# First attention layer of a diffusion trunk: the query's quarter swap goes from VectorE to small SBUF transfers, and the chunk products are spread anew

## The chip, the core and the metric

One NeuronCore of one Trainium2 chip runs the whole program. The metric is the device time of one execution in microseconds. Three runs of the kernel before took 2476.61 to 2477.92 us, median 2477.8. The engines are named as in the profile: PE (TensorE matmul), PEld (its weight load), DVE (VectorE), ACT (ScalarE), POOL (GpSimd), SP (SyncE). SPq and ACTq are the DMA issues of SP and ACT.

## The reference, cut to what matters

The trunk has four layers over 256 latent and 256 context tokens with 1024 features, in f32. Layer 0 and layer 3 are differential attention, layer 1 retention, layer 2 neighbourhood attention, and each is followed by a SwiGLU feed-forward. The change touches the mixer of layer 0:

```python
def axial_rope(x, rows, cols):
    ...
    x1, x2 = x32[..., : d // 2], x32[..., d // 2:]
    return jnp.concatenate([x1 * cos - x2 * sin, x1 * sin + x2 * cos], axis=-1).astype(x.dtype)

def diff_attention(hx, hz, w_qkv, w_o, lam_p, subln_g, lam_init, rows, cols, need_ctx):
    ...
    qx = axial_rope(qx, rows, cols)
    kx = axial_rope(kx, rows, cols)
    ...

def _diff_core(q, k, v, lam, scale):
    s = jnp.einsum('bqnd,bknd->bnqk', q, k).astype(F32) * scale
    p = jax.nn.softmax(s, axis=-1)
    b, n, tq, tk = p.shape
    p = p.reshape(b, n // 2, 2, tq, tk)
    a = p[:, :, 0] - lam * p[:, :, 1]
    return jnp.einsum('bhqk,bkhe->bqhe', a.astype(v.dtype), v)
```

Each head has 64 features, so the rotation pairs feature p with feature p +- 32. Beside it the modulation `silu(cond) @ w_ada + b_ada` is needed (`ada_mod`): 48 chunks of 128 outputs for each layer, each for the latent and for the context condition.

## The kernel before, in words

Features lie on the 128 partitions, tokens on the free axis (columns 0 to 255 latent, 256 to 511 context). Every weight matrix comes as "units" of 128x1024 values (512 KB) through a ring of four slots: SP loads `w_raw` (L420), ACT rounds it to `w_hi` (L1198), POOL subtracts to `w_lo` (L589), PE multiplies three times (hi*hi, hi*lo, lo*hi) per 128x128 block, so one unit at 512 columns is 24 matmuls.

Attention of layer 0 runs in eight tiles t of 128 features (two heads and their differential partner). For each tile PE computes the query unit into bank 6 and the key unit into bank 7, turns the weights of tile t-1 (`turn`), multiplies them with the values (`weighted`, copies by ACT L1389), and then scores tile t (`score`, six banks in the order 0, 1, 2, 4, 5, 3). Between them stands `mean_square` of tile t-1, and the last score needs a bank that DVE frees with `subnorm` of tile t-1 (L2044, semaphore `y_ready`).

DVE's order in a tile is written out by hand (`tile_da`): weights of t-1 (`weights_`, L2022 to L2037), rotation of q, rotation of k, row maxima of the scores (L2009, L2012), `subnorm` and `low` of t-1. A rotation (`rotate`, L1983) is four multiplies of 32 partitions each (L1987), which take the query from PSUM at the swapped partitions and write `rot`, one multiply of 128 partitions in PSUM (L1990) and one add into `qT` or `kT` (L1991). ACT's order is: exponentials of t-1, `value_rows`, the copy of the query's context half into `qT` (L1439), the same for the key (L1442, when PE has done the key unit), the copies of the turned weights, two weight units (`ahead`), and `high` of t-1.

In the gaps of this order DVE also works off the modulation products of layer 0 (`rest_products`, L1733): chunks 16 to 39, two products each, 48 in all, each over 128x1024 values, followed at group ends by a small sum (`ada_sums`, L1668). `ADA_VALUES`, `ADA_TILE`, `ADA_TAIL` and `ADA_PROJECT` say how many stand where; `ADA_GROUPS` says which chunk is loaded into which slot and together with which others. SP issues these loads between the weight loads (L434, `ada_rest_load`).

ACT issues two more transfers in this layer: after tile 0 the small table `rpb_rows` (L1465), and after tile 1 `rpb_skew` (L1470), which writes the table 64 times over into DRAM for the bias of layer 2, in rows of 508 bytes.

After the tiles comes the output projection (`project`): five units at 512 columns, then three units on the latent half alone, and then the same three on the context half, each of which waits until DVE has added the residual of its latent half (`x_new`, L1763).

Of the kernel before, what the change touches and what calls it, by code (L numbers as in the profile page):

```python
# [20 lines left out]
ALU = mybir.AluOpType  # L21
# [32 lines left out]
ADA_GROUPS = ((16, 0, (16, 17, 0, 4, 1, 5)), (22, 1, (2, 6, 3, 7)), (26, 0, (3,)), (27, 1, (7, 20, 21)),  # L54
              (30, 0, (3, 7)), (32, 1, (20, 21, 22)), (35, 0, (20, 23)), (37, 1, (12, 13, 14)))
ADA_MIXER = 40
ADA_VALUES = 4
ADA_TILE = ((0, 1, 2), (1, 1, 1), (1, 1, 2), (1, 1, 2), (1, 1, 2), (1, 1, 2), (1, 1, 2), (1, 1, 2))
ADA_TAIL = 8
ADA_PROJECT = (1, 1, 1, 1, 1, 1)  # L60
LOOPED = 4
# [80 lines left out]
class Layer:  # L142


    def __init__(self, sem, li, first_unit):
# [10 lines left out]
        self.first = (5 if self.kind != 1 else 6) if self.zq else KT  # L156
        self.half_done = sem(f"half_done_{li}")
        self.v_done = sem(f"v_done_{li}")
        self.v_act = sem(f"v_act_{li}")
        self.v_dve = sem(f"v_dve_{li}")  # L160
        self.s_done = sem(f"s_done_{li}")
        self.osq_ready = sem(f"osq_ready_{li}")
        self.oms_done = sem(f"oms_done_{li}")
        self.ors_ready = sem(f"ors_ready_{li}")
        self.y_ready = sem(f"y_ready_{li}")
# [12 lines left out]
        else:  # L178
# [5 lines left out]
            self.a_ready = sem(f"a_ready_{li}")  # L184
            self.t_done = sem(f"t_done_{li}")
            self.aT_ready = sem(f"aT_ready_{li}")
            self.vst_ready = sem(f"vst_ready_{li}")
# [44 lines left out]
def trunk(nc, xT_in, cond_in, weights, ada_w, ada_b, gains, final_g, lam_in, subln_in, decay_in,  # L232
          rpb_in, da_rope_in, ret_rope_in, ret_exp_in, na_mask_in, ident_in, out, layers=DEPTH):
    with ExitStack() as ctx:
# [173 lines left out]
        def _(sp):  # L408
# [99 lines left out]

            sp.wait_ge(plan[0].pv_done, KT)
            ada_rest_load(7)  # L510

            def bias_load(L, t, slot, reused):
# [667 lines left out]
        def _(act):  # L1180
# [162 lines left out]
            def attention(L):  # L1343
# [86 lines left out]
                def tile_da(t, c, i, place):  # L1430
# [6 lines left out]
                    if L.zq:  # L1437
                        act.wait_ge(unit_used, t * 2 + (n + 1))
                        nc.scalar.activation(qT[:, SEQ:TOK], bank[6][:, SEQ:TOK], ACT.Copy, scale=DA_DIM ** -0.5)\  # L1439
                            .then_inc(L.qk_act, 1)  # L1440
                    act.wait_ge(unit_used, t * 2 + (n + 2))
# [201 lines left out]
        def _(dve):  # L1643
# [339 lines left out]
            def rotate(src, dst, table):  # L1983
# [7 lines left out]
                return V.tensor_tensor(out=dst, in0=src, in1=rot[:, :], op=ALU.add)  # L1991

            def attention(L, e0):
                n = L.n + KT
# [81 lines left out]

                def tile_da(t, place, extra=(0, 0, 0)):
                    if place:
                        rest_products(extra[0])
                        weights_(t - 1)  # L2080

                    dve.wait_ge(unit_used, t * 2 + (n + 1))
                    if L.zq:
                        dve.wait_ge(L.qk_act, t * 2 + 1)
                    rotate(bank[6][:, 0:SEQ], qT[:, 0:SEQ], 0).then_inc(L.qk_dve, 1)
                    rest_products(extra[1])
                    dve.wait_ge(L.qk_act, t * (1 + L.zq) + (1 + L.zq))

                    dve.wait_ge(L.qk_dve, t * 2 + 1)
                    rotate(bank[7][:, 0:SEQ], kT[:, 0:SEQ], 2).then_inc(L.qk_dve, 1)  # L2090
                    rest_products(extra[2])
                    maxima(t, 0, range(2))
                    if place:
                        subnorm(t - 1, da_banks(L)[0])
                    maxima(t, 0, range(2, L.banks))
                    if place:
                        low(t - 1, da_banks(L)[0])
# [14 lines left out]
                else:  # L2112
                    tile_da(0, 0)
                    tile_da(1, 1)
                    with own.loop((KT - 2) // 2, 2 * (1 + 4)) as i:
                        for s in range(2):
                            tile_da(i * 2 + (2 + s), 1)
                weights_(KT - 1)
                if L.li == 0:
                    rest_products(ADA_TAIL)  # L2120
                subnorm(KT - 1, LAST_O)
# [305 lines left out]
```

## Time and profile before

| | us |
|---|---|
| median of 3 runs | 2477.8 |
| the profiled execution | 2478.16 |
| its span, first to last instruction | 2476.4 |
| PE busy in the span | 2417.1 (98%) |
| DVE busy | 1276.4 (52%) |
| ACT busy | 999.6 (40%) |
| POOL busy | 1111.5 (45%) |
| mean granted clock | 0.995 |
| tiles 0 to 7 of layer 0's attention | about 84 to 254 |
| its projection, up to the feed-forward | about 254 to 309 |

PE is busy nearly everywhere, but the shares are a mean over stages. In layer 0's attention DVE is nearly as full as PE. The slices of the page show DVE at 0.8 to 0.9 for the first 300 us and at 0.1 to 0.7 later. The granted clock is given as a share of full speed: 1.00 is 2.4 GHz and 0.50 is 1.2 GHz.

### The profile page before, as it was taken

How to read it: one execution, taken by the hardware profiler on the slowest of the kernel's cores; microseconds unless marked ns; L12 is line 12 of the kernel's file. 1: busy time of each engine (PE TensorE's matmuls, PEld its weight loads, DVE VectorE, ACT ScalarE, POOL GpSimd, SP SyncE). 2: the span in 40 equal slices, each digit the busy share in tenths (PEclk: the TensorE clock that was granted, in tenths of full speed). 3: DMA queues.
4: the chain of work that ended last, by engine and by line, in shares of the span. 5: the costliest groups of instructions: out<-in, count | busy, mean ns of one | idle time of the engine just before them, and what ended most of it. 6: DMA issues, size and time to landing. Idle time of an engine off the chain costs nothing.

```text
span 2476.4 us, 37125 instructions
## 1 busy us (share of the span) xinstructions
PE 2417.1 (98%) x12236; PEld 1976.8 (80%) x12236; DVE 1276.4 (52%) x2243; ACT 999.6 (40%) x2004; POOL 1111.5 (45%) x839
## 2 busy tenths in 40 slices
PE   8999999999999999999999999999999999998998
PEld 3566788888887777788888887778888888777998
DVE  8988876647233322247664243665666424465211
ACT  3466442332333332333323244664323324465553
POOL 0432444445443334334445434223544544435996
PEclk9999999999999999999999999999999999999999
DMA  8363345546322222235555324222555532322654
GB/s 338 111 102 110 126 163 203 199 166 222 104 87 77 74 70 86 84 103 204 189 187 192 115 73 111 78 84 94 203 203 197 184 104 92 96 75 89 192 186 128
DMA packets 119715, 340.61 MB, mean 138 GB/s; under 512 B 35537, under 2 KB 40401, under 8 KB 118993
## 3 DMA queue, kind: packets, MB, share of 16 engines
q1 hardware_dynamic: 111602, 333.97, 41.1%
q10 hardware_dynamic: 8032, 5.52, 1.5%
q8 instruction: 55, 0.90, 0.2%
q14 instruction: 26, 0.21, 0.0%
HBM read 334.76 MB, written 4.69 MB: 137 GB/s over the span
## 4 chain that ended last, share of the span: by engine, by line
issue 45%; PE 32%; POOL 18%; DVE 2%; DMA 1%; ACT 1%; SPq 1%; POOLq 1%; DVEq 0%; ACTq 0%
PE low_banks L596 28%; POOL w_lo L589 18%; PE high_banks L596 4%; DVE tmp L1804 1%; DVE h_lo L1812 0%; DMA ada_first<-in_ada_w 0%; DMA w_raw<-in_weights 0%; ACT w_hi L1198 0%; POOLq L588 0%; DVE ssum_rstd L1660 0%; POOLq L583 0%; SPq L466 0%; SPq L420 0%; DVE dump L1680 0%; SPq L434 0%
## 5 line engine op out<-in xcount | busy, mean ns | idle before, releaser
L589 POOL TENSOR_TENSOR w_lo<-w_raw,w_hi 128x512 fp32r<-128x512 f32 x832 | 1111.1, 1362 | 1345.8 <-ACT w_hi L1198 1345.2
L596 PE MATMUL low_banks<-h_hi,w_hi 128*128 128x512 f32 (+1 forms) x1792 | 644.1, 359 | 12.2 <-DVE h_lo L1812 8.4
L1198 ACT ACTIVATE w_hi<-w_raw 128x512 fp32r<-128x512 f32 x832 | 474.1, 624 | 418.3 <-PE low_banks L596 209.7
L596 PE MATMUL low_banks<-h_lo,w_hi 128*128 128x512 f32 (+1 forms) x1792 | 634.5, 354 | 0.0
L596 PE MATMUL low_banks<-h_hi,w_lo 128*128 128x512 f32 (+1 forms) x1792 | 634.4, 354 | 0.0
L596 PEld LDWEIGHTS low_banks<-h_hi,w_hi 128*128 128x128 f32 x1792 | 339.8, 190 | 68.7 <-issue 13.3
L1660 DVE SCALAR_TENSOR_TENSOR ssum_rstd<-ada_raw,high_banks 128x1024 f32<-128x1024 f32 x304 | 370.7, 1219 | 41.8 <-DMA ada_raw<-in_ada_w 32.9
L596 PEld LDWEIGHTS low_banks<-h_lo,w_hi 128*128 128x128 f32 x1792 | 340.0, 190 | 47.6 <-issue 1.9
L596 PEld LDWEIGHTS low_banks<-h_hi,w_lo 128*128 128x128 f32 x1792 | 339.9, 190 | 46.2
L1572 ACT ACTIVATE lnm<-low_banks 128x512 f32<-128x512 f32 (+1 forms) x88 | 47.8, 543 | 429.6 <-PE low_banks L596 429.5
L2250 DVE TENSOR_TENSOR tmp<-low_banks,lnm 128x512 f32<-128x512 f32 (+1 forms) x88 | 55.0, 625 | 290.0 <-ACT lnm L1572 286.3
L596 PE MATMUL high_banks<-h_hi,w_hi 128*128 128x512 f32 (+1 forms) x384 | 147.9, 385 | 1.1 <-DVE qT L1991 1.1
L596 PE MATMUL high_banks<-h_lo,w_hi 128*128 128x512 f32 (+1 forms) x384 | 144.0, 375 | 0.0
L596 PE MATMUL high_banks<-h_hi,w_lo 128*128 128x512 f32 (+1 forms) x384 | 143.6, 374 | 0.0
L596 PE MATMUL high_banks<-u_hi,w_hi 128*128 128x256 f32 (+1 forms) x424 | 141.2, 333 | 0.5 <-POOL w_lo L589 0.5
L596 PE MATMUL high_banks<-u_hi,w_lo 128*128 128x256 f32 (+1 forms) x424 | 140.6, 332 | 0.0
L596 PE MATMUL high_banks<-u_lo,w_hi 128*128 128x256 f32 (+1 forms) x424 | 140.5, 331 | 0.0
L596 PE MATMUL low_banks<-u_hi,w_lo 128*128 (+2 forms) x352 | 127.8, 363 | 0.0
L596 PE MATMUL low_banks<-u_lo,w_hi 128*128 (+2 forms) x352 | 127.8, 363 | 0.0
L596 PE MATMUL low_banks<-u_hi,w_hi 128*128 (+2 forms) x352 | 127.8, 363 | 0.0
L1763 DVE SCALAR_TENSOR_TENSOR xT<-high_banks,mod,xT 128x256 f32<-128x256 f32 x52 | 24.6, 479 | 174.2 <-PE high_banks L596 174.0
L2255 DVE TENSOR_TENSOR u_lo<-tmp,u_hi 128x512 f32 (+2 forms) x88 | 65.9, 749 | 60.8 <-ACT u_hi L1577 56.0
(246 smaller groups left out, 3691.9 us busy)
## 6 DMA issues: line engine op xcount, KB each, us to landing
w_raw<-in_weights SPq DMA_DIRECT2D x424, 512.0 KB, 3.7
ada_raw<-in_ada_w SPq DMA_DIRECT2D x152, 512.0 KB, 3.9
ada_first<-in_ada_w SPq DMA_DIRECT2D x24, 512.0 KB, 9.6
ada_rest<-in_ada_w SPq DMA_DIRECT2D x9, 512.0 KB, 7.6
bias<-rpb_skew SPq DMA_DIRECT2D x64, 64.0 KB, 2.4
v_all<-in_ada_w SPq DMA_DIRECT2D x7, 512.0 KB, 6.1
rpb_skew<-rpb_rows ACTq DMA_DIRECT2D x1, 3556.0 KB, 31.7
cond_l<-in_cond SPq DMA_DIRECT2D x3, 1024.0 KB
```

The source lines that it names most:

```text
L589: nc.gpsimd.tensor_tensor(out=w_lo[:, r, part], in0=w_raw[:, r, part], in1=w_hi[:, r, part], op=ALU.subtract).then_inc(lo_ready, 1)
L596: return nc.tensor.matmul(dst, lhsT, rhs, start=start, stop=stop, **kw)
L1198: nc.scalar.activation(w_hi[:, r, part], w_raw[:, r, part], ACT.Copy).then_inc(hi_ready, 1)
L1572: nc.scalar.activation(lnm[:, 0:L.W], bank[2 * s][:, 0:L.W], ACT.Silu)\
L1660: last = V.scalar_tensor_tensor(out=dump, in0=w, scalar=1.0, in1=cond[:, c, :], op0=ALU.mult, op1=ALU.mult, accum_out=ada_sum[:, r, c:c + 1])
L1763: return V.scalar_tensor_tensor(out=x, in0=src[:, COLS[c]], scalar=gate_of(L, which, m, c), in1=x, op0=ALU.mult, op1=ALU.add)
L1804: V.scalar_tensor_tensor(out=tmp[:, m % 2, COLS[c]], in0=xT[:, m, COLS[c]], scalar=amp[:, L.par, q % 2, m, c:c + 1], in1=rstd[:, COLS[c]], ...
L2250: V.tensor_tensor(out=tmp[:, s, 0:L.W], in0=bank[2 * s + 1][:, 0:L.W], in1=lnm[:, 0:L.W], op=ALU.mult).then_inc(L.u_free, 1)
L2255: V.tensor_tensor(out=row(u_lo, j, L.W), in0=tmp[:, s, 0:L.W], in1=row(u_hi, j, L.W), op=ALU.subtract).then_inc(L.u_lo_ready, 1)
```

## The change

In layer 0, and there only, ACT now copies all 512 columns of the query out of PSUM, scaled, into `qT`, waits for its own copy, and issues four transfers within SBUF, of 32 partitions x 256 f32 (32 KB) each, that write the swapped latent half into `rot`. DVE waits for all four (`swapped_in`) and then rotates with three operations on SBUF operands in place of six. The key's rotation stays. The 48 chunk products are spread differently, chunks 37 to 39 go to other slots, and their loads are tied to other events. A few semaphores that nobody used are dropped.

```diff
-              (30, 0, (3, 7)), (32, 1, (20, 21, 22)), (35, 0, (20, 23)), (37, 1, (12, 13, 14)))
+              (30, 0, (3, 7)), (32, 1, (20, 21, 22)), (35, 0, (20, 23)), (37, 1, (21, 22)), (39, 0, (20,)))
-ADA_VALUES = 4
-ADA_TILE = ((0, 1, 2), (1, 1, 1), (1, 1, 2), (1, 1, 2), (1, 1, 2), (1, 1, 2), (1, 1, 2), (1, 1, 2))
-ADA_TAIL = 8
-ADA_PROJECT = (1, 1, 1, 1, 1, 1)
+ADA_VALUES = 3
+ADA_TILE = ((0, 0, 1, 1), (1, 1, 1, 0), (1, 1, 1, 1), (1, 1, 1, 1), (1, 1, 1, 1), (1, 1, 1, 1), (1, 1, 1, 2),
+            (1, 1, 1, 2))
+ADA_TAIL = (1, 9)
+ADA_PROJECT = (1, 1, 1, 1, 0, 0)
...
-            sp.wait_ge(plan[0].pv_done, KT)
+            sp.wait_ge(ada_done, 35)
             ada_rest_load(7)
+
+            sp.wait_ge(ada_done, 36)
+            ada_rest_load(8)
...
                     if L.zq:
                         act.wait_ge(unit_used, t * 2 + (n + 1))
-                        nc.scalar.activation(qT[:, SEQ:TOK], bank[6][:, SEQ:TOK], ACT.Copy, scale=DA_DIM ** -0.5)\
-                            .then_inc(L.qk_act, 1)
+                        nc.scalar.activation(qT[:, :], bank[6][:, :], ACT.Copy, scale=DA_DIM ** -0.5).then_inc(L.qk_act, 1)
+
+                        act.wait_ge(L.qk_act, t * 2 + 1)
+                        for quarter in range(4):
+                            a, b = 32 * quarter, 32 * (quarter ^ 1)
+                            act.dma_start(rot[a:a + 32, :], qT[b:b + 32, 0:SEQ]).then_inc(L.swapped_in, 16)
...
+            def rotate_swapped(x):
+
+                V.tensor_tensor(out=rot[:, :], in0=rot[:, :], in1=da_rope[:, 3, :], op=ALU.mult)
+                own(V.tensor_tensor(out=x, in0=x, in1=da_rope[:, 2, :], op=ALU.mult))
+                return V.tensor_tensor(out=x, in0=x, in1=rot[:, :], op=ALU.subtract)
...
-                def tile_da(t, place, extra=(0, 0, 0)):
+                def tile_da(t, place, extra=(0, 0, 0, 0)):
                     if place:
                         rest_products(extra[0])
                         weights_(t - 1)
-
-                    dve.wait_ge(unit_used, t * 2 + (n + 1))
+                    rest_products(extra[1])
                     if L.zq:
-                        dve.wait_ge(L.qk_act, t * 2 + 1)
-                    rotate(bank[6][:, 0:SEQ], qT[:, 0:SEQ], 0).then_inc(L.qk_dve, 1)
-                    rest_products(extra[1])
+                        dve.wait_ge(L.swapped_in, t * 64 + 64)
+                        rotate_swapped(qT[:, 0:SEQ]).then_inc(L.qk_dve, 1)
+                    else:
+                        dve.wait_ge(unit_used, t * 2 + (n + 1))
+                        rotate(bank[6][:, 0:SEQ], qT[:, 0:SEQ], 0).then_inc(L.qk_dve, 1)
+                    rest_products(extra[2])
                     dve.wait_ge(L.qk_act, t * (1 + L.zq) + (1 + L.zq))
                     ...
-                    rest_products(extra[2])
+                    rest_products(extra[3])
                     maxima(t, 0, range(2))
...
+                if L.li == 0:
+                    rest_products(ADA_TAIL[0])
                 weights_(KT - 1)
                 if L.li == 0:
-                    rest_products(ADA_TAIL)
+                    rest_products(ADA_TAIL[1])
```

## Rows read from the trace of the kernel before

**Rows 1.** Busy time of each engine in one stretch: PE, PEld, DVE, ACT, POOL, clock, DMA.

```profile
150.00:172.00 22.00, 20.87 (x90) 14.27 (x89) 19.46 (x36) 14.00 (x34) 6.91 (x4) 1.00 0.26 83
```

**Rows 2.** DVE's timeline, tile 3 and the start of tile 5: start, duration, [idle before].

```profile
149.55 1.72 DVE L1987 TENSOR_TENSOR rot<-high_banks,da_rope 32x256 f32<-32x256 f32 x4
151.30 0.43 DVE L1990 TENSOR_TENSOR high_banks<-high_banks,da_rope 128x256 f32<-128x256 f32 x1
151.77 0.42 DVE L1991 TENSOR_TENSOR qT<-high_banks,rot 128x256 f32<-128x256 f32 x1
152.11 1.22 DVE L1733 SCALAR_TENSOR_TENSOR dump<-ada_first,cond 128x1024 f32<-128x1024 f32 x1
...
154.16 1.72 DVE L1987 TENSOR_TENSOR rot<-high_banks,da_rope 32x256 f32<-32x256 f32 x4 [0.82 <-DVE dump L1733]
...
158.68 2.16 DVE L1733 SCALAR_TENSOR_TENSOR dump<-ada_first,cond 128x1024 f32<-128x1024 f32 x1
...
162.09 0.74 DVE L2044 SCALAR_TENSOR_TENSOR tmp<-low_banks,subln,ssum_rstd 128x512 f32<-128x512 f32 x1
...
193.16 1.22 DVE L1733 SCALAR_TENSOR_TENSOR dump<-ada_first,cond 128x1024 f32<-128x1024 f32 x1 [4.22 <-DMA v_all<-in_ada_w]
```

**Rows 3.** ACT's timeline in tile 3: the query's and the key's copy.

```profile
148.59 0.36 ACT L1439 ACTIVATE qT<-high_banks 128x256 f32<-128x256 f32 x1
153.69 0.39 ACT L1442 ACTIVATE kT<-high_banks 128x256 f32<-128x256 f32 x1 [4.74 <-PE high_banks L596]
```

**Rows 4.** Timelines of PE and PEld: scores, query units, the projection's stop.

```profile
113.89 2.08 PE L596 MATMUL low_banks<-kT,qT 64*128 64x512 f32 x4 [2.25 <-DVE kT L1991]
...
136.08 1.13 PE L596 MATMUL low_banks<-kT,qT 64*128 64x512 f32 x4
...
142.47 0.19 PEld L596 LDWEIGHTS high_banks<-h_hi,w_hi 128*128 128x128 f32 x1 [0.76 <-POOL w_lo L589]
...
162.89 1.12 PE L596 MATMUL low_banks<-kT,qT 64*128 64x512 f32 x2 [1.13 <-DVE tmp L2044]
...
185.55 2.07 PE L596 MATMUL low_banks<-kT,qT 64*128 64x512 f32 x2 [2.27 <-DVE tmp L2044]
...
187.54 0.29 PEld L596 LDWEIGHTS high_banks<-h_hi,w_hi 128*128 128x128 f32 x1 [1.50 <-issue]
...
254.28 0.19 PEld L596 LDWEIGHTS high_banks<-y_hi,w_hi 128*128 128x128 f32 x1 [0.76 <-issue]
...
298.71 0.58 PE L596 MATMUL low_banks<-y_hi,w_hi 128*128 128x256 f32 x1 [3.46 <-DVE xT L1763]
```

**Rows 5.** ACT's own transfers in this layer: start and issue; KB, us to landing.

```profile
119.92 0.71 ACTq L1470 DMA_DIRECT2D rpb_skew<-rpb_rows  x1
...
rpb_skew<-rpb_rows ACTq DMA_DIRECT2D x1, 3556.0 KB, 31.7
...
rpb_rows<-in_rpb ACTq DMA_DIRECT2D x1, 13.6 KB, 1.8
```

**Rows 6.** DMA issues of the first 20 us, with KB and us to landing.

```profile
da_rope<-in_da_rope ACTq DMA_DIRECT2D x1, 512.0 KB, 7.1
...
logit<-in_decay SPq DMA_DIRECT2D x1, 4.0 KB, 14.1
```

**Rows 7.** DMA queue of ACT, 148 to 150 us: packets, MB, share.

```profile
q10 hardware_dynamic: 31, 0.01, 3.9%
```

**Rows 8.** Busy time and clock in a stretch after PE's stop at 183 to 185 us.

```profile
189.00:192.00 3.00, 3.00 (x9) 2.33 (x8) 0.00 (x0) 1.59 (x5) 0.00 (x0) 0.50 0.99 339
```

**Rows 9.** DVE adds of 128x256 on SBUF, POOL idle, then POOL at work.

```profile
299.13 0.43 DVE L1792 TENSOR_TENSOR ssum_rstd<-ssum_rstd,tmp 128x256 f32<-128x256 f32 x1
...
307.70 1.51 DVE L1792 TENSOR_TENSOR ssum_rstd<-ssum_rstd,tmp 128x256 f32<-128x256 f32 x1
```

**Rows 10.** DVE in the projection: one of the last products, and the sum.

```profile
289.80 2.31 DVE L1733 SCALAR_TENSOR_TENSOR dump<-ada_rest,cond 128x1024 f32<-128x1024 f32 x1
...
296.10 1.10 DVE L1668 TENSOR_TENSOR mod<-ada_sum,bias_ada 128x6 f32<-128x6 f32 x1
```

More of the change, by code:

```diff
@@ L156, in __init__ @@
         self.first = (5 if self.kind != 1 else 6) if self.zq else KT
-        self.half_done = sem(f"half_done_{li}")
+        if self.zq:
+            self.half_done = sem(f"half_done_{li}")
         self.v_done = sem(f"v_done_{li}")
@@ L161, in __init__ @@
         self.s_done = sem(f"s_done_{li}")
-        self.osq_ready = sem(f"osq_ready_{li}")
-        self.oms_done = sem(f"oms_done_{li}")
-        self.ors_ready = sem(f"ors_ready_{li}")
+        if self.kind != 2:
+            self.osq_ready = sem(f"osq_ready_{li}")
+            self.oms_done = sem(f"oms_done_{li}")
+            self.ors_ready = sem(f"ors_ready_{li}")
         self.y_ready = sem(f"y_ready_{li}")
@@ L185, in __init__ @@
             self.t_done = sem(f"t_done_{li}")
+            if self.kind == 0 and self.zq:
+                self.swapped_in = sem(f"swapped_in_{li}")
             self.aT_ready = sem(f"aT_ready_{li}")
```

## The prediction, made before the change was run

> **What bounds the kernel now.** I read the page first: PE is busy 98% of the span, so a change to DVE's work pays only where PE waits for DVE. The busy times by stretch show where that can be: in the middle of layer 0's attention DVE is busy 19.46 of 22 us beside PE's 20.87 [rows 1]. Then I read the timelines of that stage engine by engine, with S for the start of a tile's query unit on PE. Tile 3 has S = 142.47, and the tile's last score runs at 162.89 after a stop of 1.13 us for DVE's `subnorm`; it takes 1.05 us, so the next S is 163.94 and a tile lasts 21.47 us. From 187.54 to the projection's first unit at 254.28 there are three tiles in 66.74 us where 3 x 21.47 = 64.4 would do, and from 142.47 to 187.54 two tiles in 45.07 us where 42.9 would do [rows 4]. The excess of 2.3 and 2.1 us belongs to two events. In tile 4 a stop of 2.27 us was followed by half the granted clock [rows 4, 8]. In tile 5 a product of chunk 27 waited 4.22 us for its load [rows 2]. The stop of 1.13 us had no such sequel. Last, the projection has one stop of 3.46 us, for the residual that DVE adds late [rows 4].
>
> **The quarter swap on DVE.** It removes four multiplies of 32 partitions (1.72 us), keeps one multiply (0.43) and one add (0.42), and adds one multiply of 128x256 [rows 2]. All three operands are now in SBUF. Such an add took 0.43 us with POOL idle and 1.51 with POOL at work [rows 9]. POOL is idle when tiles 1 to 7 rotate the query, so I take three times 0.43 = 1.3 us in place of 2.6, and up to 3.3 us in tile 0.
>
> **The swap as a path.** In tile 3 ACT starts the query's copy at S + 6.1 [rows 3]. At 512 columns I take 0.6 us for it (twice the columns of the 0.36 row, less its fixed part). Then four issues; the large transfer on this queue took 0.71 us to issue [rows 5], and I take 0.4 for a small one, an estimate. From issue to landing the small table took 1.8 us [rows 5]. So the last swap lands at about S + 6.7 + 1.2 + 1.8 = S + 9.7. No transfer of this shape, SBUF to SBUF, is in the trace: below 1.8 us is open, above it I go to 4 us. DVE has meanwhile done the product that used to follow, waits 1.4 us, rotates until S + 11.0, does one product (1.22) and is at the key at S + 12.3, where it used to start at 154.16 = S + 11.7 because the key unit ends there [rows 2, 3]. The key's rotation ends at about S + 14.9, and PE's scores begin at S + 15.1. That fits just. One product less then stands before the maxima, `subnorm` comes 0.9 us earlier, and the next S is at 20.5 rather than 21.47. What was moved beside it is only ACT's wait for its own copy, behind which the key's copy is queued; ACT sat idle 4.74 us before that one [rows 3], so it costs nothing in tiles 2 to 7.
>
> **Tile 2, the term that decides.** After tile 1 ACT issues `rpb_skew` at 119.92. It lands 31.7 us later, at 151.6 [rows 5], and 31 packets of it were still served between 148 and 150 us [rows 7]. Tile 2's four swaps are issued at about 128 on the same queue, q10. The first 20 us show what a queue does to a small transfer behind large ones: 4 KB on SP's queue took 14.1 us to land, while 512 KB issued after it on ACT's queue took 7.1 [rows 6]. So a queue serves in order, and the other queue goes past it. The Trainium skill says so too (page "DMA: Bandwidth & Descriptors", section "Queues, rings and completion order"): each engine takes a ring's descriptors in order, and ACT has one row of rings.
>
> By this the swaps land at about 151.8, not at 130. DVE then needs 1.35 + 1.25 + 2.65 us for the query, a product and the key: 157.1. PE's scores start there, where they started at 136.08 [rows 4]: 21.1 us late. DVE has nothing else to do, since the wait stands ahead of everything in its order; PE goes through turn and weighted sums until 136 and then stands still. Where the clock fell after a stop it was 0.50, that is 1.2 GHz [rows 8]. In tile 1, after 2.25 us, four scores' row lasts 2.08 us where tile 2's lasts 1.13, and in tile 4 the scores' row 2.07 [rows 4], with the unit behind it still at 0.50 [rows 8]: one to some three us each. I take 1.2, since much of what follows waits on ACT and DVE in any case: +22.3, between +19 and +26.
>
> **Tiles 0 and 1.** One product fewer ahead of tile 0 pays for the swap's latency; tile 1's swap lands after DVE is free, and the key is ready at the same time as before. -0.3, between -1.5 and +2.
>
> **Tiles 3 to 5.** The product of chunk 27 moves from ahead of the weights to behind the query's rotation, later than its landing, so the 4.22 us go; with one product less before the maxima the stop of tile 4 falls below the 2.27 that halved the clock. From 142.47 to the start of tile 6, 68.8 us in all, become three times 20.5 and 0.6 for a sum: -6.7, between -7.3 and -2.
>
> **Tiles 6 and 7.** Here two products remain before the maxima while the key is ready 0.6 us later, and in tile 6 a sum falls between them, which beside POOL took 1.10 us in place of 0.17 [rows 10]. The stop grows from 1.13 to about 2, or 2.8 with the sum, where the clock may fall. +2, between +1.2 and +4.9.
>
> **Tail and loads.** Nine products in place of eight, and the last two of them wait for a group of loads that can only start when chunk 34 is done (about 6 us to land, 5 us of products in between). PE has 0.7 us to spare. +0.4, between 0 and +1.5. SP's queue gets one wait more, with nothing due behind it until the projection.
>
> **Projection.** Two products of 2.31 us and the late sum of 1.10 no longer stand before the last residuals [rows 10]. That is 4.6 us and more against a stop of 3.46 us with 2.3 us of half clock behind it [rows 4]; what is late next is PE's own third half unit. -4.3, between -5 and -2.
>
> **Sum.** 22.3 - 0.3 - 6.7 + 2.0 + 0.4 - 4.3 = +13.4 us. The profiled execution took 2478.16 us, 0.4 above the median of the runs, so 2491.6 for it and 2491.2 for the median. I say 2491. The other layers are unchanged: layer 3 has no context queries and takes the old rotation.
>
> **Rivals.**
> *The transfers pass each other.* If the swap of tile 2 didn't wait for `rpb_skew`, tile 2 would gain 0.7 as the others: 2477.8 - 9.6 = 2468. For it: the swap is small, and both transfers are cut into pieces for 16 engines whose ends are counted one by one. Against it: the 14.1 us of 4 KB [rows 6]. The same page and section of the Trainium skill add that completion is not in order for each issuing engine when a transfer uses fewer engines than the one before; both transfers here divide by 16, so this would not help. Chance 0.12.
> *The wait takes the place of the work.* The transfers pass, but land 2 us later than I say in every tile. Then DVE's saved 1.3 us is spent on waiting, the key is ready after PE wants it, and each tile lasts about 22.3: tile 2 +0.8, tiles 3 to 5 -1.3, tiles 6 and 7 +5, tiles 0 and 1 +2, the rest -3.9, in all +2.6: 2480. It decides from a landing of 3 us after the last issue. This is also the case in which the change doesn't do what it says. Chance 0.06.
> *In order, and the queue holds ACT itself.* ACT could be stopped at the issue itself while its queue is full. The key's copy and the turned weights would then come late too, but they need some 5 us from about 149, and the key is not rotated before 157 anyway. This lies in the likeliest case's upper half.
>
> **How the numbers follow.** The likeliest case, in-order service, has 0.82. Its terms at their low ends give +6, at likely high ends +20. The range 2484 to 2499 holds nearly all of it, and what it leaves out are the rivals and a little of its ends. 0.2% of this kernel is 5 us, about what a measurement can tell from no change; the likeliest case is slower by more than that. Faster 0.12 (first rival), same 0.06 (second rival), slower 0.82.
>
> **What would show it.** In the changed kernel's DVE timeline: one wait of about 22 us in tile 2 for a DMA into `rot`, ending near 152, and waits of 1 to 2 us in the other tiles. On PE: a stop of about 20 us before tile 2's scores, then clock 0.50. Landing of the swaps: about 2 us in seven tiles, over 20 us in one. No wait of 4 us for chunk 27, and no stop of 3.46 us in the projection. I am wrong if the swap of tile 2 lands within 5 us, or if it lands before `rpb_skew` does.

## The result and the profile after

| | before | after |
|---|---|---|
| median, us | 2477.2 | 2513.43 |
| runs | 5, 2476.56 to 2477.92 | 5, 2513.03 to 2516.55 |
| profiled execution, us | 2478.16 | 2515.35 |
| its span, us | 2476.4 | 2513.6 |
| mean granted clock | 0.995 | 0.986 |

The change makes the kernel slower: ratio 1.0145, interval 1.0134 to 1.0157. It is 37.2 us between the two profiled executions, where I had forecast +13.4. The direction was right, and the size was far outside the range.

The starts of the query units, S, cut the 37.2 us into the terms of the sum. The rows of before are in [rows 4]; in after, S is 128.49 for tile 2, 172.25 for tile 3, 194.85, 221.18, 243.22 and 268.13 for tiles 4 to 7, and 292.71 for the projection.

| | forecast | measured |
|---|---|---|
| tiles 0 and 1 | -0.3 | +7.5 |
| tile 2 | +22.3 | +22.3 |
| tiles 3 to 5 | -6.7 | +2.1 |
| tiles 6 and 7 | +2.0 | +6.5 |
| tail and projection | -3.9 | -1.2 |

So the big term was exact, and everything around it was worse than forecast. First tile 2, in the timeline of ACT in after (start, duration, engine, line, [idle before]; ACTq is an issue of a transfer):

```profile
127.43 0.68 ACTq L1482 DMA_DIRECT2D rpb_skew<-rpb_rows  x1
...
134.91 0.58 ACT L1447 ACTIVATE qT<-high_banks 128x512 f32<-128x512 f32 x1
135.52 14.62 ACTq L1452 DMA_DIRECT2D rot<-qT  x4
150.25 0.38 ACT L1454 ACTIVATE kT<-high_banks 128x256 f32<-128x256 f32 x1 [14.76 <-issue]
...
180.42 2.45 ACTq L1452 DMA_DIRECT2D rot<-qT  x4
```

`rpb_skew` was issued at 127.43 and landed after 28.2 us (31.7 in [rows 5]), at 155.6. The four swaps of tile 2 stood behind it. In tile 3 the same four issues take 2.45 us, in tile 2 they take 14.62: ACT itself was held while it issued. DVE in after:

```profile
90.53 1.04 DVE L2007 TENSOR_TENSOR rot<-rot,da_rope 128x256 f32<-128x256 f32 x1 [5.44 <-DMA rot<-qT]
...
93.01 1.37 DVE L2009 TENSOR_TENSOR qT<-qT,rot 128x256 f32<-128x256 f32 x1
...
117.57 1.10 DVE L1680 TENSOR_TENSOR mod<-ada_sum,bias_ada 128x8 f32<-128x8 f32 x1
...
156.49 1.41 DVE L2007 TENSOR_TENSOR rot<-rot,da_rope 128x256 f32<-128x256 f32 x1 [19.51 <-DMA rot<-qT]
...
184.21 0.42 DVE L2007 TENSOR_TENSOR rot<-rot,da_rope 128x256 f32<-128x256 f32 x1 [4.77 <-DMA rot<-qT]
...
207.35 0.43 DVE L2007 TENSOR_TENSOR rot<-rot,da_rope 128x256 f32<-128x256 f32 x1 [4.31 <-DMA rot<-qT]
...
253.73 0.43 DVE L2007 TENSOR_TENSOR rot<-rot,da_rope 128x256 f32<-128x256 f32 x1 [2.31 <-DMA rot<-qT]
...
258.69 1.96 DVE L1745 SCALAR_TENSOR_TENSOR dump<-v_all,cond 128x1024 f32<-128x1024 f32 x1
...
260.69 1.10 DVE L1680 TENSOR_TENSOR mod<-ada_sum,bias_ada 128x6 f32<-128x6 f32 x1
261.83 2.25 DVE L1745 SCALAR_TENSOR_TENSOR dump<-ada_first,cond 128x1024 f32<-128x1024 f32 x1
```

In all eight tiles DVE waits for the swap, 47.2 us together, 19.51 of it in tile 2 and never under 2.31. The forecast had 1 to 2 us in the other tiles. What this does to PE, in its timeline (rows of PE and of its weight load PEld, both in after):

```profile
121.41 2.08 PE L604 MATMUL low_banks<-kT,qT 64*128 64x512 f32 x4 [3.70 <-DVE kT L2003]
...
162.66 2.08 PE L604 MATMUL low_banks<-kT,qT 64*128 64x512 f32 x4 [6.49 <-DVE kT L2003]
...
212.53 1.13 PE L604 MATMUL low_banks<-kT,qT 64*128 64x512 f32 x4 [2.51 <-DVE kT L2003]
...
266.13 2.07 PE L604 MATMUL low_banks<-kT,qT 64*128 64x512 f32 x2 [3.09 <-DVE tmp L2062]
...
291.37 1.42 PE L604 MATMUL low_banks<-kT,qT 64*128 64x512 f32 x2 [1.94 <-DVE tmp L2062]
```

```profile
94.43 0.29 PEld L604 LDWEIGHTS high_banks<-h_hi,w_hi 128*128 128x128 f32 x1 [5.85 <-DVE qT L2009]
...
151.17 0.50 PEld L604 LDWEIGHTS low_banks<-aT,v_st 128*128 128x128 f32 x2 [10.43 <-ACT aT L1397]
...
172.25 0.29 PEld L604 LDWEIGHTS high_banks<-h_hi,w_hi 128*128 128x128 f32 x1 [1.50 <-issue]
...
336.29 0.19 PEld L604 LDWEIGHTS low_banks<-y_hi,w_hi 128*128 128x128 f32 x1 [1.51 <-DVE xT L1775]
```

PE stands in tiles 0, 1, 2, 4, 6 and 7 for results that DVE has late. In tile 2 it stands twice: 10.43 us (PEld's row) for the turned weights, which ACT could not copy while it was held at the issue, and 6.49 us (PE's row) for the key. PEld's rows give a stop as some tenths of a us longer than PE's (4.11 where PE has 3.70), so a figure is compared only with one of the same engine. After such stops the clock is at half, here after the stop that ends at 162.66, and for the most part at the projection's start:

```profile
162.00:172.00 10.00, 9.34 (x18) 3.86 (x18) 5.72 (x11) 4.74 (x12) 0.00 (x0) 0.50 0.00 1
...
292.00:296.00 4.00, 4.00 (x11) 2.62 (x10) 3.45 (x7) 4.00 (x16) 0.00 (x0) 0.57 0.28 111
```

(Busy time of PE, PEld, DVE, ACT, POOL, then clock, DMA share, GB/s, as in [rows 1].)

### The profile page after: what moved, and what is told of

The parts are those of the page before. It is cut to its first block, busy times and chain, and to the rows that moved or that the text cites. A ratio compares the mean times of both kernels' runs of the same rounds, so it can differ in the third digit from the quotient of the medians.

```text
span 2513.6 us, 37140 instructions
## 1 busy us (share of the span) xinstructions
PE 2433.5 (97%) x12236; PEld 1983.4 (79%) x12236; DVE 1269.7 (51%) x2220; ACT 1001.5 (40%) x2004; POOL 1101.5 (44%) x839
## 4 chain that ended last, share of the span: by engine, by line
issue 53%; PE 23%; POOL 22%; DVE 2%; POOLq 1%; ACT 1%; DVEq 0%; ACTq 0%
POOL w_lo L597 22%; PE low_banks L604 20%; PE high_banks L604 3%; DVE h_lo L1824 0%; DVE tmp L1816 0%; POOLq L596 0%; POOLq L591 0%; DVE ssum_rstd L1672 0%; ACT w_hi L1206 0%; DVE mod L1680 0%; ACT L1579 0%; DVE ssum_rstd L1804 0%; DVE xT L1775 0%; ACT h_hi L1242 0%; ACT lnm L1230 0%
## 5 line engine op out<-in xcount | busy, mean ns | idle before, releaser
L604 PEld LDWEIGHTS high_banks<-h_hi,w_hi 128*128 128x128 f32 x384 | 73.9, 192 | 32.4 <-issue 11.6
## 6 DMA issues: line engine op xcount, KB each, us to landing
rpb_skew<-rpb_rows ACTq DMA_DIRECT2D x1, 3556.0 KB, 28.2
```

Source lines behind the costliest of these rows:

```text
L604: return nc.tensor.matmul(dst, lhsT, rhs, start=start, stop=stop, **kw)
```

## The experiments

All were timed beside the kernel before on the same chip; its median was 2476.9 us in the first four, 2476.9 in the next four and 2477.8 in the last three. All medians are in a table behind the last one.

**The spread without the swap.** The new counts and load groups, the old rotation, no transfers (cut):

```diff
-                        nc.scalar.activation(qT[:, :], bank[6][:, :], ACT.Copy, scale=DA_DIM ** -0.5).then_inc(L.qk_act, 1)
-
-                        act.wait_ge(L.qk_act, t * 2 + 1)
-                        for quarter in range(4):
-                            a, b = 32 * quarter, 32 * (quarter ^ 1)
-                            act.dma_start(rot[a:a + 32, :], qT[b:b + 32, 0:SEQ]).then_inc(L.swapped_in, 16)
+                        nc.scalar.activation(qT[:, SEQ:TOK], bank[6][:, SEQ:TOK], ACT.Copy, scale=DA_DIM ** -0.5)\
+                            .then_inc(L.qk_act, 1)
...
+                    dve.wait_ge(unit_used, t * 2 + (n + 1))
                     if L.zq:
-                        dve.wait_ge(L.swapped_in, t * 64 + 64)
-                        rotate_swapped(qT[:, 0:SEQ]).then_inc(L.qk_dve, 1)
...
+                        dve.wait_ge(L.qk_act, t * 2 + 1)
+                    rotate(bank[6][:, 0:SEQ], qT[:, 0:SEQ], 0).then_inc(L.qk_dve, 1)
```

> The new spread of products, slots and loads, with the old rotation by six VectorE operations and no swap transfers. Theory (the transfers are what costs): faster than before, 2469 us (2464 to 2474): no wait for chunk 27, no 3.46 us stop in the projection. Rival (the new spread itself costs, by the two products and the sum ahead of the maxima in tiles 6 and 7 and the one ahead of the query's rotation): 2480 or more.

It took 2471.65 us, ratio 0.9979 (0.9966 to 0.9991): faster, as expected. PEld in its profiled execution, which took 2475.11 us, 3.5 above the median of its runs:

```profile
113.40 0.50 PEld L604 LDWEIGHTS low_banks<-kT,qT 64*128 64x128 f32 x4 [5.24 <-DVE kT L1999]
...
144.75 0.19 PEld L604 LDWEIGHTS high_banks<-h_hi,w_hi 128*128 128x128 f32 x1 [0.76 <-POOL w_lo L597]
...
165.32 0.19 PEld L604 LDWEIGHTS high_banks<-h_hi,w_hi 128*128 128x128 f32 x1 [0.76 <-POOL w_lo L597]
...
228.13 0.49 PEld L604 LDWEIGHTS low_banks<-kT,qT 64*128 64x128 f32 x2 [2.70 <-DVE tmp L2058]
```

From 144.75 to 165.32 is one tile of 20.57 us, against 21.47 in before. That is the gain that I had put down to the swap and the spread together, and the spread has all of it. By the terms of the sum this execution has +2.0 in tiles 0 and 1 (the stop of 5.24 is in tile 1), +0.3 in tile 2, -7.1 in tiles 3 to 5, +4.4 in tiles 6 and 7, and -2.6 behind them.

**The swap without the spread.** The old counts, with every product where it stood before (the new tuples only have one place more), the old load groups, and `rpb_skew` behind the last swap (cut):

```diff
-ADA_TILE = ((0, 0, 1, 1), (1, 1, 1, 0), (1, 1, 1, 1), (1, 1, 1, 1), (1, 1, 1, 1), (1, 1, 1, 1), (1, 1, 1, 2),
-            (1, 1, 1, 2))
-ADA_TAIL = (1, 9)
+ADA_TILE = ((0, 0, 1, 2), (1, 0, 1, 1)) + ((1, 0, 1, 2),) * 6
+ADA_TAIL = (0, 8)
...
```

> The swap by transfers with the old spread, slots and loads, and rpb_skew moved behind the last swap. Theory (the swap's latency pushes the key's rotation to S + 15.6, and two products behind it push subnorm past PE's tolerance): 2505 us (2498 to 2512), PE stops over 2 us and clock 0.50 in most tiles. Rival (the new spread is to blame for the later tiles): 2485 or less, below the run with the new spread.

2514.4 us, ratio 1.0135 (1.0109 to 1.0161): 2.4 above the expected range, with one of its four runs at 2505.33. The rival, 2485 or less, is out. It is slower than before by 37 although nothing stands ahead of its swaps. PEld waited 13.1 us for `subnorm` (five times) and 7.4 us once for `low` at the start of the projection, which is the collision of the next but one run. That run has the new counts and `rpb_skew` in the same place and takes 2503.3, so the swap costs some 11 us more under the old counts.

**No transfers at all.** After without the four swaps; DVE waits for ACT's copy only, so the rotated query is not the right one (cut):

```diff
-                        act.wait_ge(L.qk_act, t * 2 + 1)
-                        for quarter in range(4):
-                            a, b = 32 * quarter, 32 * (quarter ^ 1)
-                            act.dma_start(rot[a:a + 32, :], qT[b:b + 32, 0:SEQ]).then_inc(L.swapped_in, 16)
...
-                        dve.wait_ge(L.swapped_in, t * 64 + 64)
+                        dve.wait_ge(L.qk_act, t * 2 + 1)
```

> The changed kernel without the four transfers and without the wait for them: DVE waits for ACT's copy alone and uses whatever rot holds, so the rotated query is wrong; rpb_skew stays where it is. It gives the change's arithmetic and spread at no latency. Theory: 2466 us (2461 to 2471). Rival (the copy of 512 columns by ACT, or the three SBUF operations beside POOL, cost by themselves): 2478 or more.

2469.68 us, ratio 0.9974 (0.9961 to 0.9986), as expected. Everything else of the change is in it: the copy of 512 columns, the rotation on SBUF operands, the spread. So the transfers and what waits for them cost 2513.4 - 2469.7 = 43.7 us. What they save DVE is small even when they are free: this run is 2.0 us below the spread with the old rotation, less than the scatter of either.

**`rpb_skew` behind the last swap.**

```diff
-                if L.li == 0:
-                    act.wait_ge(skew_in, 16)
-                    act.dma_start(rpb_skew, ...)
                 with own.loop((KT - 2) // 2, 2) as i:
                     ...
+                if L.li == 0:
+                    act.wait_ge(skew_in, 16)
+                    act.dma_start(rpb_skew, ...)
```

> The changed kernel, with the large transfer rpb_skew moved behind the last tile's swap on ACT's queue; nothing else. Theory (two separate losses: 22 us in tile 2 behind rpb_skew, and some 14 us from the swap's own latency of 3.8 to 5.8 us from issue to DVE, with the clock drops that it brings): 2491 us (2487 to 2495), no wait over 6 us for a DMA into rot, and no transfer issue over 1 us on ACT. Rival A (all of the loss comes from the queue, the later tiles only inherit it): 2478 or less. Rival B (the queue costs less than the stop of tile 2 shows, since work is done ahead behind it): 2500 or more.

2503.26 us, ratio 1.010 (1.0083 to 1.0117): only 10.2 us of the 22.3 came back, and the time lies where rival B had it. The wait of 19.51 us was gone (the longest for a swap was 5.57), and another had come. DVE, and the transfers issued between 268 and 297 (KB, median us to landing):

```profile
295.89 1.22 DVE L1745 SCALAR_TENSOR_TENSOR dump<-v_all,cond 128x1024 f32<-128x1024 f32 x1 [14.22 <-DMA v_all<-in_ada_w]
```

```profile
rpb_skew<-rpb_rows ACTq DMA_DIRECT2D x1, 3556.0 KB, 37.2
v_all<-in_ada_w SPq DMA_DIRECT2D x4, 512.0 KB, 18.1
```

The chunk loads on SP's queue took 18.1 us to land, where the median of this kind in after is 5.7; a product waited 14.22, and PE waited 11.8 for `low` behind it. `rpb_skew` had been taken from ahead of the swaps and put beside the late loads. It did not stand in their queue, but the same 16 engines serve both: from 268 to 297 ACT's queue took 72.3% of their time and SP's 37.0%, which leaves none free. This expectation was wrong because I had asked only which queue the large transfer stands in. Rival B's reason, work done ahead behind the queue, is not what the trace shows; the next run puts the transfer where it meets neither.

**`rpb_skew` at the start of the projection, with a control.** The same edit of place, once in after and once in the spread without the swap:

```diff
                     lead = 0 if L.li else 3
+                    if L.li == 0:
+                        act.wait_ge(skew_in, 16)
+                        act.dma_start(rpb_skew, ...)
```

> The changed kernel with rpb_skew moved further back, to the start of the output projection on ACT's queue, so that it meets neither a swap nor the loads of chunks 35 to 39. Theory (skew_last came out at 2503 because the moved transfer held up those loads: DVE waited 14.2 us for chunk 37 and PE 11.8 us for y_lo; the queue itself costs 22 us in the changed kernel): 2489 us (2485 to 2494). Rival (the queue's net cost is only the 10 us that skew_last showed): 2500 or more.

> Control for the move: new spread, old rotation, no swaps, and rpb_skew at the start of the projection. Theory (the move by itself is nearly free): within 3 us of the run with the new spread alone, 2471 us (2468 to 2474). If the move itself helps or costs, it shows here and is taken off the other run.

2497.43 us (ratio 1.0079, 1.0063 to 1.0096) and 2480.12 (1.0007, 0.9997 to 1.0016). Both missed their ranges, the first by 3.4 us and the control by 6.1: the move was not free. In the first the projection starts at 269.41 where in after it starts at 292.71: 23.3 us less, tile 2's term and a little. The control has the same attention as the run without the move (the projection starts at 254.15 against 253.79) and still loses 8.5 us by the medians. Between the profiled executions it is 7.3, of which 6.9 lie behind the attention. In the control's trace, ACT, then PEld, then the DMA queues and landings between 272 and 300:

```profile
296.05 1.15 ACT L1206 ACTIVATE w_hi<-w_raw 128x512 fp32r<-128x512 f32 x2 [12.56 <-DMA w_raw<-in_weights]
```

```profile
301.82 0.29 PEld L604 LDWEIGHTS low_banks<-y_hi,w_hi 128*128 128x128 f32 x1 [6.30 <-DVE xT L1771]
```

```profile
q10 hardware_dynamic: 5071, 2.58, 71.5%
...
w_raw<-in_weights SPq DMA_DIRECT2D x4, 512.0 KB, 12.1
```

ACT's queue took 71.5% of the 16 engines, the weight units took 12.1 us to land instead of 3.5, ACT stood 12.56 us for one, its squares and with them the residual came late, and PE stopped 6.30 us. With these 8.5 us taken off, the swap without a queue ahead of it stands at 2489, which is the time of the theory. So moving the transfer has a price where it meets loads that are waited for, here and in the run before.

**One transfer in place of four.** After with `rpb_skew` in the projection, and there one transfer of 128x256 straight across; so the rotated query is not the right one:

```diff
-                        for quarter in range(4):
-                            a, b = 32 * quarter, 32 * (quarter ^ 1)
-                            act.dma_start(rot[a:a + 32, :], qT[b:b + 32, 0:SEQ]).then_inc(L.swapped_in, 16)
+                        act.dma_start(rot[:, :], qT[:, 0:SEQ]).then_inc(L.swapped_in, 16)
...
-                        dve.wait_ge(L.swapped_in, t * 64 + 64)
+                        dve.wait_ge(L.swapped_in, t * 16 + 16)
```

> As the run with rpb_skew at the projection, but one transfer of 128 partitions x 256 in place of four of 32, copied straight, so that the quarters are not swapped and the query comes out wrong. Same bytes, one issue of about 0.6 us in place of four in 2.44. Theory (the issues are the part of the latency that tips it): DVE starts the rotation 1.8 us earlier, and the time is 2477 us (2472 to 2483), at least 8 below the four-transfer run. Rival (landing is what costs, not the issues): within 4 us of the four-transfer run.

2481.87 us, ratio 1.0012 (1.0002 to 1.0022), inside the expected range: 15.6 below the four transfers, and 1.75 above the control without any, which is less than the scatter of either (both have runs from 2474 to 2483). The rival, that landing costs and not the issues, is out. The same bytes on the same queue between the same points cost next to nothing as one transfer. Tile 3 with four, in the run with `rpb_skew` in the projection (ACT's issue, DVE's first use), then tile 3 with one:

```profile
161.01 2.45 ACTq L1452 DMA_DIRECT2D rot<-qT  x4
...
164.81 0.43 DVE L2007 TENSOR_TENSOR rot<-rot,da_rope 128x256 f32<-128x256 f32 x1 [2.34 <-DMA rot<-qT]
```

```profile
150.19 0.48 ACTq L1450 DMA_DIRECT2D rot<-qT  x1
...
152.25 0.42 DVE L2005 TENSOR_TENSOR rot<-rot,da_rope 128x256 f32<-128x256 f32 x1 [0.59 <-DMA rot<-qT]
```

From the first issue to DVE it is 3.8 us with four and 2.1 with one. The landing takes 1.9 us for one of the four and 2.0 for the one, so the difference of 1.7 is three more issues of 0.61, less 0.1. With one issue tiles 3, 4 and 5 last 20.55, 20.56 and 20.57 us, the time of the spread alone; with four they last 21.18, 23.71 and 21.16. No run has one transfer that also swaps the quarters.

**Better counts without the swap.**

```diff
-ADA_TILE = ((0, 0, 1, 1), (1, 1, 1, 0), ..., (1, 1, 1, 2), (1, 1, 1, 2))
+ADA_TILE = ((0, 0, 1, 1), (1, 0, 0, 2), ..., (2, 1, 1, 1), (2, 1, 1, 1))
```

> New spread, old rotation, no swaps, rpb_skew in its old place, and the products of tiles 1, 6 and 7 moved within the tile: (1, 0, 0, 2) in tile 1 and (2, 1, 1, 1) in tiles 6 and 7, so that none stands ahead of tile 1's key and the fifth one of tiles 6 and 7 runs before the weights, while POOL is idle. Theory (PE's stops over 2 us and the half clock after them are what the spread still loses): 2466 us (2462 to 2470). Rival (a product costs PE the same wherever it stands in the tile): 2471 as the spread alone.

2463.28 us, ratio 0.9945 (0.9929 to 0.9962), inside the expected range, with the rival out: the fastest of all here, 13.6 us below before and 50 below after. Its only stop of over 2 us in the attention, for `subnorm` in tile 1:

```profile
116.85 0.29 PEld L604 LDWEIGHTS low_banks<-kT,qT 64*128 64x128 f32 x2 [2.65 <-DVE tmp L2058]
```

The stop of 5.24 in tile 1 and the one of 2.70 with its half clock in tile 6 are gone.

**`rpb_skew` in eight pieces, in three kernels.** The same bytes, spread over the attention so that no swap stands behind more than two of them, in after, in the kernel with better counts, and in the two together (cut):

```diff
+                    if L.li == 0 and place >= 2:
+                        act.dma_start(rpb_skew[:, bass.ds(t * 8, 8), :],
+                                      rpb_rows[:, :].unsqueeze(1).to_broadcast([7 * NA_HEADS, 8, RPB_PAD]))\
+                           .then_inc(skew_out, 16)
...
-                    act.dma_start(rpb_skew, rpb_rows[:, :].unsqueeze(1).to_broadcast([7 * NA_HEADS, GRID_W, RPB_PAD]))\
-                       .then_inc(skew_out, 16)
+                    for c in range(0, 16, 8):
+                        act.dma_start(rpb_skew[:, c:c + 8, :], rpb_rows[:, :].unsqueeze(1).to_broadcast([7 * NA_HEADS, 8, RPB_PAD]))\
+                           .then_inc(skew_out, 16)
```

> The changed kernel with one edit: rpb_skew, the 3556 KB transfer that ACT issued in one piece after tile 1, is cut into eight pieces of 444 KB with the same packets. Two stand after tile 1, and one stands behind the last swap of each tile 2 to 7, on the same queue. Theory (tile 2 waits because everything of rpb_skew stands ahead of its swaps in a queue served in order, and the rest of the loss is the swap's own path): the 22.3 us of tile 2 nearly go; two pieces after tile 1 need 2 x 4 us from about 127, so tile 2's swaps at 135 find an empty queue. 2513.4 - 22.3 = 2491, between 2487 and 2497. Tile 2's wait for the swap falls from 19.5 us to 2 to 6, and no swap takes more than 0.7 us to issue. Rival (moving the bytes costs what it saves, as in the run with rpb_skew behind the last swap, 2503): 2500 to 2506.

> The spread alone with the tuned counts (median 2463.3, no swap transfers, old rotation) and rpb_skew in the same eight pieces as in the run with the pieces. A control: it tells what the pieces cost by themselves. Theory: nothing waits for them and nothing small is queued behind them, so 2463.3, between 2461 and 2467. Rival (a moved rpb_skew costs some 8.5 us wherever it lies, as in the run that moved it to the projection): 2470 to 2474.

> The run with the pieces of rpb_skew, with the four swap transfers, and the tuned counts of products in tiles 1, 6 and 7 (1,0,0,2) and (2,1,1,1). Beside the control it gives the price of the swap through the queue once nothing stands in its way. Theory (the swap's path of 3.8 us and more from the first issue to DVE costs 17 us over the eight tiles, as between the two runs with rpb_skew in the projection, 2497.4 against 2480.1): 2463.3 + 17 = 2480, between 2475 and 2486: the change's spread with its swap stays slower than the kernel before even with its queue freed. Rival (most of those 17 us were stops by badly placed products, which the tuned counts take away): 2463 to 2472.

After with the pieces took 2493.76 us (ratio 1.0065, 1.0049 to 1.0082), inside the range of the theory (2487 to 2497) and not near the 2503 of the rival. Tile 2 lasts from 128.86 to 150.62, 21.76 us, where in after it lasts 43.76: 22.0 us back, with nothing changed in that tile but what stands ahead of its swaps, and one piece behind them. The control took 2466.65, at the upper edge of its expectation: the pieces cost some 3 us by themselves. With the swap and the better counts it is 2488.4 (1.0037, 1.0023 to 1.0051), 21.75 above that control, and 2.4 over the upper end of what I had expected. So the better counts don't cure the swap: the rival falls. In after with the pieces, tile 3 is undisturbed and tile 4 isn't. DVE and PEld:

```profile
161.19 0.43 DVE L2012 TENSOR_TENSOR rot<-rot,da_rope 128x256 f32<-128x256 f32 x1 [2.39 <-DMA rot<-qT]
...
184.62 0.42 DVE L2012 TENSOR_TENSOR rot<-rot,da_rope 128x256 f32<-128x256 f32 x1 [4.59 <-DMA rot<-qT]
```

```profile
150.62 0.19 PEld L604 LDWEIGHTS high_banks<-h_hi,w_hi 128*128 128x128 f32 x1 [0.76 <-issue]
...
171.84 0.19 PEld L604 LDWEIGHTS high_banks<-h_hi,w_hi 128*128 128x128 f32 x1 [0.76 <-issue]
...
190.88 0.50 PEld L604 LDWEIGHTS low_banks<-kT,qT 64*128 64x128 f32 x4 [4.26 <-issue]
...
197.99 0.19 PEld L604 LDWEIGHTS high_banks<-h_hi,w_hi 128*128 128x128 f32 x1 [0.76 <-issue]
```

Tile 3: swap there at 161.19 = S + 10.6, next S after 21.22 us. Tile 4: at 184.62 = S + 12.8, a stop of 4.26, scores at half clock, next S after 26.15. What differs beside them is a chunk load of 512 KB that SP issued at 180.06, while ACT was issuing the swaps (178.57 to 181.04). It isn't the piece of `rpb_skew` behind the swaps, since tile 3 has one too, and the run with `rpb_skew` in the projection has none: its tile 4 took 5.7 us from the first issue to DVE, with a load issued at 183.67 amid swaps from 182.19 on, where this one took 6.1.

| run | median, us | beside before, us |
|---|---|---|
| after | 2513.4 | +36.2 |
| swap without the spread | 2514.4 | +37.5 |
| `rpb_skew` last | 2503.3 | +26.4 |
| `rpb_skew` in the projection | 2497.4 | +20.5 |
| after, `rpb_skew` in pieces | 2493.8 | +16.0 |
| the same, better counts | 2488.4 | +10.6 |
| one transfer | 2481.9 | +4.9 |
| spread, `rpb_skew` in the projection | 2480.1 | +3.2 |
| spread alone | 2471.7 | -5.2 |
| no transfers | 2469.7 | -7.2 |
| better counts, pieces, no swap | 2466.7 | -11.2 |
| better counts, no swap | 2463.3 | -13.6 |

The swap on an unobstructed queue costs 17.3 us (2497.4 against 2480.1) or 21.8 (2488.4 against 2466.7). In the first pair `rpb_skew` still disturbs both kernels in the projection, so the two need not agree better.

## Why the prediction was right or wrong, point by point

**Tile 2 behind `rpb_skew`: right, +22.3 for +22.3.** The queue serves in order, as [rows 6] had shown for SP's queue, and the trace of after agrees with the sentence that I had taken from the Trainium skill (page "DMA: Bandwidth & Descriptors", section "Queues, rings and completion order"). `rpb_skew` landed at 155.6 and DVE had the swap at 156.5. The wait was forecast as about 22 us ending near 152, and was 19.51 ending at 156.5; tile 2 itself began 7.5 us later. That the sum fits to a tenth is partly luck: PE's scores start 34.2 us after S (162.66 less 128.49) where they started at 15.1, so the delay is 19.1 and not 21.1, and the half clock took 3.2 in this tile and not 1.2. The first rival, that the transfers pass each other, is out: the pieces and the moved `rpb_skew` each took away that wait. The third, that ACT is held at the issue, happened (14.62 us), and it was right that it lies inside the term: ACT was held until 150.1, and PE waited for the key's rotation until 162.66.

**The swap as a path: wrong, and this is the step that failed.** I had "0.4 for a small one, an estimate" for an issue and 1.8 for the landing. The landing was 1.9. An issue is 0.61, so the four take 2.45 and not 1.6, and the last swap is there 3.8 us after the first issue and not 3.0. In a quiet tile (tile 3 of the run with the pieces) DVE then starts at S + 10.6 instead of S + 9.7, the key is rotated 0.7 later, and "that fits just" no longer fits: PE's scores start at S + 15.76, not 15.1, behind a stop of 0.58. A tile lasts 21.2 us and not 20.5. The path had no slack, and the 4 us to which I let the landing go widened none of the terms that hang on it. In place of the landing the issue was at fault; the second rival named the right mechanism with a threshold on the wrong quantity, and it came beside the queue, not in place of it. How much hangs on this step the run with one transfer shows: one issue in place of four gives 15.6 us back, where the whole sum was 23.8 us short (37.2 against 13.4). The 0.8 us by which I had the path too short are not 15.6 us by themselves; they became so because nothing in the path could take them up, and because swaps that are issued for 2.45 us meet loads that a single one does not meet (next two points).

**Tiles 3 to 5: the same term, +2.1 for -6.7.** The wait of 4.22 us for chunk 27 did go, as forecast, and the spread alone has tiles of 20.57. But three tiles of after last 70.97 us where I had 62.1. Tile 3 has 22.60, its first 3.75 us still at half clock from the stop in tile 2 (I had 1.2 us for all of that). Tile 4 has 26.33. ACT and SP in after:

```profile
201.58 2.45 ACTq L1452 DMA_DIRECT2D rot<-qT  x4
```

```profile
203.07 0.34 SPq L439 DMA_DIRECT2D ada_first<-in_ada_w  x1
```

A load of 512 KB was issued while ACT was still issuing the four; DVE had the swap at S + 12.5, and the stop of 2.51 us was followed by half the clock. I had not asked what else the 16 engines carry in the moment of the swap. With one transfer the load comes 1.5 us after the only issue (172.24 against 170.75), the swap is there in 2.1 us, and the tile lasts 20.56. That these two slow each other is what the timing of the traces shows (tile 4 of after, of the run with the pieces and of the one with `rpb_skew` in the projection); no run moved the load alone.

**Tiles 0 and 1: +7.5 for -0.3.** "up to 3.3 us in tile 0" was in the working for the rotation beside POOL, and it took 3.9 (1.04, 1.48 and 1.37), but I never carried it into the term. A weight load that SP issued at 86.15 fell among the four issues of tile 0, and DVE had the swap 5.8 us after the first. So the key unit, which needs the query's bank, started after a stop of 5.85 us where there was 1.55 before (PEld's rows), at half clock. In tile 1 the sum beside POOL (1.10) fell between the query's and the key's rotation, and the stop of [rows 4] grew from 2.25 to 3.70. The spread has part of this by itself: without the swap PEld stops 5.24 in tile 1 (4.11 in after) and not in tile 0, and the two tiles take 2.0 us more than before. The forecast had no stop for the spread in tile 1 beyond that of before.

**Tiles 6 and 7: right mechanism, too small, +6.5 for +2.0.** Forecast was a stop of 2, or 2.8 with the sum, where the clock may fall. It was 3.09 in tile 6 with the sum of 1.10 and products of 1.96 and 2.25 ahead of `subnorm`, and the clock fell; in tile 7 it was 1.94. The spread without the swap has, in PEld's view, 2.70 in tile 6 and 1.47 in tile 7, where after has 3.49 and 2.35: the products do most, +4.4 of the term in the spread alone, and the later key adds 0.8 and 0.9 to the stops.

**Projection and tail: -1.2 for -3.9.** The stop of 3.46 us for the residual is 1.30 in the same view (1.51 in PEld's). What I took as next, PE's own work, is not next; ACT's and DVE's residual chain still is. From the start of the projection to the end of the span, before needs 2222.1 us, the spread alone 2219.5 and after 2220.9. So the residual gave 2.6, and in after 1.4 of it went again, with the projection's first units at clock 0.57 behind the stop of tile 7.

**What was left out.** The terms were right to stand apart, but their errors, where they had one, all had one sign, and a good part of them is the same swap path. Not all: the spread alone is worse than forecast by 2.3 us in tiles 0 and 1, 2.4 in tiles 6 and 7 and 1.3 behind them. The range was too narrow by its own working as well: the high ends of the terms add up to +30.4, where the range ends at +21. Even they don't reach +37.2. Had I costed an issue by the one that the rows showed, ACT's large one with 0.71, the path would have been 3.9 us and the quiet tile's time right.

## What to carry to other kernels

A transfer that takes the place of work costs its issues, one after the other on the issuing engine, before it costs its landing: here four issues of 0.61 us for 128 KB cost 15.6 us over eight tiles against one issue for the same bytes. Ask of a small urgent transfer three things: what stands ahead of it in its queue, what else the DMA engines carry in that moment, and whether the path had slack at all; and when a large transfer is moved out of its way, ask the same of what it is moved beside. The swap had little to win here: with no transfer at all the kernel is 2.0 us below the spread with the old rotation, within the scatter, so nearly all of the gain was in the counts. If several terms of a sum hang on one unmeasured price, move them together when the range is made.

## What the runs showed of the hardware that was not expected

- The engine that issues can be held behind a large transfer on its own queue: four issues took ACT 14.62 us behind `rpb_skew` (3556 KB in rows of 508 bytes) and 2.45 otherwise, and ACT did none of its other work in that time. Whether the bytes or the number of rows do it, no run tells.
- An issue of 32 partitions within SBUF takes 0.61 us on ACT, and one of 128 partitions 0.48. The landing is 1.9 and 2.0 us. With a load of 512 KB issued on SP's queue amid the four, DVE had the swap 5.7 to 6.1 us after the first issue in place of 3.8.
- Queues keep their order but share the 16 engines: beside `rpb_skew` on ACT's queue, 512 KB on SP's queue took 12.1 us to land instead of 3.5 (weights) and 18.1 instead of 5.7 (chunks). The Trainium skill (page "DMA: Bandwidth & Descriptors", section "Queues, rings and completion order") says that an engine takes turns between its queue rows, packet by packet. The slowed loads agree with that, though no row here shows the turns themselves.
